# Prompt attention: both exponentials of a step ahead of the value copies, in tiles 4 to 7

## The reference, cut to what matters

```python
s_c = einsum(qg, kc);  p_c = masked_softmax(s_c, c_end <= q_pos)          # compressed blocks
s_s = einsum(qg, selected keys);  p_s = masked_softmax(s_s, k_pos <= q_pos)
s_w = einsum(qg, window keys);    p_w = masked_softmax(s_w, (dist >= 0) & (dist < WINDOW))
o = g0 * (p_c @ vc) + g1 * (p_s @ v_slc) + g2 * (p_w @ v_win)             # gates g
```

## Time and profile before

| | |
|---|---|
| median of 3 runs | 2177.78 us (2173.7 to 2178.57) |
| the profiled execution | 2175.42 us, of which the span is 2173.8 us |
| PE busy | 2087.7 us (96%) |
| DVE, ACT, POOL busy | 1160.8, 627.8, 168.7 us |
| chain that ended last | PE 88%, DVE 5%, ACT 4%, issue 1%, DMA 1% |
| line 1266 (exponentials) | 128 instructions, 88.9 us, on the chain 1% |
| line 1252 (value copies) | 148 instructions, 80.5 us, on the chain 1% |
| mean granted TensorE clock | 0.986 |

### The profile page before, as it was taken

One profiled execution on the slowest core, in us unless ns is written; L12 is line 12 of the kernel. 1 busy time (PEld: TensorE's weight loads), 2 busy tenths in 40 slices (PEclk: granted clock), 3 DMA queues, 4 the chain that ended last, 5 costly groups with the idle time before them and its releaser, 6 DMA issues.

```text
span 2173.8 us, 37161 instructions
## 1 busy us (share of the span) xinstructions
PE 2087.7 (96%) x15252; PEld 1186.4 (55%) x15252; DVE 1160.8 (53%) x2353; ACT 627.8 (29%) x1414; POOL 168.7 (8%) x280
## 2 busy tenths in 40 slices
PE   8999999899998897989998999999999999999999
PEld 6445566799997785444444444444444444444443
DVE  2035664376675556877656446354544545463635
ACT  5014553122231224766644222111111111111020
POOL 3000000122221101211203000000000000000000
PEclk9999999999998998999999999999999999999999
DMA  6100112100002731000036601111111111111112
GB/s 178 39 0 20 29 30 82 79 4 13 14 10 57 199 113 55 11 6 6 6 117 195 199 1 39 39 39 39 39 39 39 39 39 39 39 39 39 39 39 82
DMA packets 96886, 115.73 MB, mean 53 GB/s; under 512 B 32243, under 2 KB 68020, under 8 KB 96654
## 3 DMA queue, kind: packets, MB, share of 16 engines
q1 hardware_dynamic: 90702, 101.82, 14.9%
q10 hardware_dynamic: 4480, 7.34, 1.2%
q0 software_dynamic: 1536, 4.20, 0.6%
HBM read 104.75 MB, written 12.64 MB: 54 GB/s over the span
## 4 chain that ended last, share of the span: by engine, by line
PE 88%; DVE 5%; ACT 4%; issue 1%; DMA 1%; ACTq 0%; POOL 0%; POOLq 0%; DVEq 0%
PE psum L1396 81%; PE psum L1844 2%; PE psum L1728 1%; ACT arena L1266 1%; PE psum L1901 1%; ACT arena L1252 1%; DVE arena L2503 1%; DVE arena L2529 1%; DVE arena L2353 1%; PE psum L1646 0%; PE psum L1406 0%; ACTq L1217 0%; PE psum L2094 0%; DVE psum L2500 0%; DVE arena L2584 0%
## 5 line engine op out<-in xcount | busy, mean ns | idle before, releaser
L1396 PE MATMUL psum<-arena 64*64 64x64 f32 (+10 forms) x12296 | 1844.2, 347 | 51.6 <-ACT arena L1266 20.2
L1396 PEld LDWEIGHTS psum<-arena 64*64 64x64 f32 (+5 forms) x12296 | 959.8, 151 | 824.1 <-issue 652.0
L2701 DVE TENSOR_TENSOR arena<-arena,psum 128x512 f32<-128x512 f32 x51 | 35.1, 687 | 318.5 <-PE psum L1396 318.5
L1369 ACT ACTIVATE arena<-psum 128x512 f32<-128x512 f32 x51 | 30.3, 594 | 437.4 <-PE psum L1396 344.7
L1358 ACT ACTIVATE arena<-arena 128x512 f32<-128x512 f32 x64 | 40.2, 628 | 274.2 <-DVE arena L2715 168.0
L918 POOL TENSOR_TENSOR arena<-arena,m_lev 128x256 f32<-128x256 f32 x82 | 65.4, 798 | 574.3 <-DVE arena L2334 377.0
L1252 ACT ACTIVATE arena<-psum 128x512 f32<-128x512 f32 (+1 forms) x148 | 80.5, 596 | 68.3 <-PE psum L1844 60.3
L2503 DVE TENSOR_REDUCE arena<-psum 128x1 f32<-128x640 f32 (+7 forms) x128 | 84.6, 703 | 15.1 <-PE psum L1396 13.5
L1266 ACT ACTIVATE arena<-psum,arena 128x640 f32<-128x640 f32 (+7 forms) x128 | 88.9, 703 | 9.6 <-DVE arena L2503 9.5
L2353 DVE TENSOR_TENSOR arena<-arena,psum 128x512 f32<-128x512 f32 x65 | 44.6, 686 | 74.1 <-PE psum L1396 73.4
L1844 PEld LDWEIGHTS psum<-ident,arena 128*128 128x128 f32 x528 | 58.0, 143 | 45.5 <-issue 22.6
(11 more groups left out here) (314 smaller groups left out, 1787.6 us busy)
## 6 DMA issues: line engine op xcount, KB each, us to landing
arena<-in_w_up_dram SPq DMA_DIRECT2D x7, 2048.0 KB, 7.4
arena<-in_w_down_dram SPq DMA_DIRECT2D x7, 2048.0 KB, 7.8
arena<-in_cache_slc_kv_dram SPq DMA_DIRECT2D x96, 128.0 KB, 2.6
arena<-in_cache_cmp_kv_dram SPq DMA_DIRECT2D x72, 128.0 KB, 3.3
arena<-in_x_prompt_dram SPq DMA_DIRECT2D x16, 512.0 KB, 13.6
arena<-in_cache_cmp_kv_dram ACTq DMA_DIRECT2D x56, 128.0 KB, 3.4
arena<-in_w_in_dram SPq DMA_DIRECT2D x13, 512.0 KB, 3.8
arena<-in_w_in_dram SPq DMA_DIRECT2D x2, 2048.0 KB, 12.5
```

The lines of the kernel that those rows point to most:

```text
L1396: return nc.tensor.matmul(out, lhsT, rhs, start=start, stop=stop)
L2701: tt(u2, t_sb, bank_of(6), ALU.add).then_inc(sem("u_sum"), 1)
```

## The change

In a score step that is not the compressed one, in tile 4 or later, with no turn of queries before the next score step and exactly one value step there, both exponentials get keys x + 0.1 and x + 0.2, ahead of the copies of that value step (which is at x + 1). All other steps keep their keys. The copies keep their order among themselves, and so do the exponentials. Nothing is changed on PE, DVE, POOL or SP, and no wait is added or taken away.

```diff
             nxt = next((y for y in range(x + 1, len(order)) if order[y][0] == "S"), len(order))
             vs = [y for y in range(x + 1, nxt) if order[y][0] == "V"]
+            turns_queries = any(order[y][0] == "q" for y in range(x + 1, nxt))
+            if e[2] != "c" and UNITS_A[e[1]][0] >= WINDOW // P and not turns_queries and len(vs) == 1:
+                act_order += [(x + 0.1, ("E", e[1], e[2], 0)), (x + 0.2, ("E", e[1], e[2], 1))]
+                continue
             act_order.append((vs[0] + 0.5 if vs else x, ("E", e[1], e[2], 0)))
```

## The result

The changed kernel took **2165.62 us** (median of 5 runs, 2162.40 to 2165.74), where the kernel before took 2177.78 (5 runs by then, 2173.70 to 2182.02); ratio 0.9946, 95% interval 0.9931 to 0.9960. The profiled execution took 2165.64 us, with a span of 2164.0, against 2175.42 and 2173.8.

A forecast was written before the change was run, and what follows sets the result against it. PE was taken as the bound in tiles 4 to 7, waiting for exponentials queued behind early copies on ACT. Terms 1.88 + 3.52 + 0.99 + 0.67 + 0.30 made about 7.4: 2177.8 - 7.4 = 2170.4 us, range 2166.5 to 2176.5.

The forecast's parts named there:

- its term: Predicted gains of units 8 to 15, in order: 1.88, 1.49, 0.99, 0.87, 0.67, 0.53, 0.30 and 0.63 us.
- M + 0.86: In a 640-column step, the first exponential starts 0.86 us after M, the start of the pair of maxima.
- M + 1.63: In a 640-column step, the second exponential starts 1.63 us after the start of the pair of maxima.
- P at M + 2.57: In 640-column steps, P, the start of piece 0 of the next scores, comes at 2.57 instead of 3.20: gain 0.63 us.
- 2.90 at 768: In 768-column steps of unit 10, piece 0 of the next scores comes at 2.90 against 3.38: gain 0.48 us.
- 3.27 and 3.65: Piece 0 of the next scores at 896 and 1024 columns, against 3.59 and 3.81: gains 0.32 and 0.16 us.
- DVE's mask: First steps of units 9, 11, 13: mask ends at 945.65, so the next maxima start at most 0.24 us earlier.
- a sum of 7.36: Gain over tiles 4 to 7: 1.88 + 3.52 + 0.99 + 0.67 + 0.30 us, all taken to the kernel's end.
- The unknown cost: Exponentials of 640 to 1024 columns running while DVE reads the other strip: at most 0.01 us each, taken as 0.
- the third rival: Exponential and maximum take turns on PSUM in the changed steps: 5.0 us slower, 2182.8 us; chance 5%.
- The first: Gains of units 8, 10, 12, 14 (3.84 us) turn into longer stalls at unit ends: 2174.3 us; chance 15%.
- The second: In the changed steps the order changes and nothing moves: exponentials start as now or PE waits for copies; 2177.8 us, 5%.

The follow-up runs named there:

- experiment 11: The changed kernel once more, unchanged, 12 runs: 2167.82 us, ratio 0.9968 to the kernel before.
- 4: The changed kernel again, unchanged, 5 runs: 2166.53 us, ratio 0.9962 to the kernel before.
- 5: The changed kernel with only the first exponential ahead of the two copies, the second behind them: 2183.27 us, ratio 1.0035 to the kernel before.
- 7: The changed kernel, with the second exponential straight behind the first also in two-value steps of tiles 4 to 7 without a turn of queries next: 2164.80 us.
- 12: The changed kernel with the second exponential also moved in two-value steps, run once more, 5 runs: 2161.99 us, ratio 0.9933 to the kernel before.
- 2: The changed kernel with the move only in its 10 steps of 640 columns: 2169.12 us, ratio 0.9978 to the kernel before.
- 3: The changed kernel with the move only in its 6 steps of 768 to 1024 columns: 2173.17 us, ratio 0.9992 to the kernel before.
- 6: The changed kernel with the move also in one-value steps of tiles 4 to 7 with a turn of queries next: 2170.33 us, ratio 0.9975.
- 9: The changed kernel without the limit to tiles 4 to 7, so 17 more steps in tiles 0 to 3: 2169.04 us, ratio 0.9968.
- 10: The changed kernel with a PE pad, 28 repeated transposes in 3.2 us at the end of prompt attention: 2170.63 us, ratio 0.9981 to the kernel before.

## Why the prediction was wrong, and where it was right

**The steps.** The mechanism held, and each unit's gain came within 0.06 us of its term. M + 0.86 was measured, M + 1.63 came at 1.65, P at M + 2.57 in 640 steps came at 2.57 to 2.58, 2.90 at 768 at 2.92, 3.27 and 3.65 at 896 and 1024 at 3.28 and 3.65. The steps are 3.82 apart (3.81). DVE's mask is the next bound in unit 9: the gain there is 1.51, not the 1.79 that it would be without it (0.54 + 0.63 + 0.62). The stretch gained 7.33 us for a sum of 7.36. The sum has a slip: 3.17, 3.20 and 3.19 less 2.57 each make 1.85 in unit 8 and not 1.88, so it should read 7.33. That this is the measured figure to the last digit is luck, for single units are off by up to 0.06 in both directions.

**The unknown cost.** The overlap of exponential and running maximum was taken at nothing. Grouped by shape over the stretch of the changed kernel:

```profile
L1270 ACT ACTIVATE arena<-psum,arena 128x640 f32<-128x640 f32 x40 | 31.6, 794 | 13.3 <-DVE arena L2507 13.3
L2507 DVE TENSOR_REDUCE arena<-psum 128x1 f32<-128x640 f32 x40 | 31.1, 819 | 4.4 <-PE psum L1400 3.8
...
L1270 ACT ACTIVATE arena<-psum,arena 128x1024 f32<-128x1024 f32 x8 | 9.0, 1122 | 5.4 <-DVE arena L2507 5.4
```

The means, 794, 819 and 1122 ns, were 799, 820 and 1121 in the old order. That refutes the third rival. It could have been ruled out beforehand: the prediction says that no row of the kernel before shows the overlap at 640 columns and more, but at 1024 columns one does. The pair of maxima runs until 1048.48, and the first exponential, 0.89 us of it beside the second maximum, takes as long as the one that follows alone at 1048.68 (1.10 us):

```profile
1047.59 1.10 ACT L1266 ACTIVATE arena<-psum,arena 128x1024 f32<-128x1024 f32 x1
```

The Trainium skill ("PSUM — Partial Sum Buffer", "Specifications (TRN2)") says that ScalarE and VectorE reach PSUM side by side at full bandwidth if they don't collide in a bank. The trace agrees with it, now at 640 to 1024 columns.

**The other rivals.** The first falls with the table by unit: units 8, 10, 12 and 14 kept their 3.77 us, and the stall stayed at 0.66. The second falls with all of it.

**The step that failed** is "the forecast is for the median: 2177.8 - 7.4". It carried a gain that was right to 0.03 us on a base that wasn't.
- The three runs of before were a poor sample of it: 91 runs have a median of 2175.95. The profiled execution (2175.4), from which I moved the forecast away by 2.4 us, was the better base: 2175.95 - 7.33 = 2168.6, beside 2167.82 for experiment 11.
- The five runs of the changed kernel were a lucky sample of that: 2164.5 in the mean at a clock of 0.9878, where 22 runs have 2166.8 at 0.9870. Their median, 2166.53, would have stood just inside the range, at its lower edge. In the profiled execution the forecast of 2168.0 was missed by 2.4 us, and 2.48 stand ahead of the stretch, where the change does nothing. Within one kernel the time falls by 1.2 to 2.0 us for each 0.001 of mean granted clock (a straight line through the runs of each set with at least nine). At a clock of 0.986 the lines of the sets give 2174.6 to 2175.0 for the kernel before and 2167.1, 2169.1 and 2168.7 for the three sets of the changed one: 5.5 to 7.9 us, around the 7.33. Two of the three are sets of five runs with clocks of 0.987 to 0.989, so their lines are carried on beyond them; the twelve runs of experiment 11 against their own rounds give 2174.9 - 2168.7 = 6.2.
- The range was built on the cost terms alone. A run of one kernel stands anywhere within 10 to 14 us (2162.4 to 2172.0 for the changed kernel, 2170.8 to 2184.8 for the kernel before), and three of them don't fix a median to 2 us; that scatter belonged in the range.

**What stays open.** In the plain means the changed kernel is 9.2 us faster (22 and 91 runs), with a standard error of about 0.7, 1.9 more than its stretch. The surplus sits mostly in the sets of five runs: beside the gain of their stretches, the differences of the means from their own rounds are 5.5 (the first five), 2.3, 0.4, 1.3 and 5.2 us (experiments 4, 5, 7 and 12) in these, and between -0.7 and 1.2 in the six sets of nine to twelve runs (2, 3, 6, 9, 10 and 11, where for 10 the pad is counted in). The difference goes with the clock, and part of the clock's is shown to be chance (650 to 700 us). Whether the higher clock and the 2.4 us shorter sample stage belong to the new order isn't settled, nor why the stages behind it give up to all of that back: with the PE pad, standing 3 us later took about those 3 us, but no run moved it by the whole 7 with PE at work.

## What to carry to other kernels

In an in-order queue, ask of each entry how soon its result is wanted, and put the one that PE waits for ahead of the one whose result is used a step later; but move a whole group (half the move cost 8 us), and only where something long stands before the next use of what the moved entry frees (about 1 us lost per step otherwise). Work out such a move from one step's timeline: start of the maximum, its duration, the queue behind it, the release. Then put the forecast on a base with the run-to-run scatter in it, because here the scatter of the base was larger than the error of the whole sum.

## What the runs showed of the hardware that I had not expected

- The same instructions between 650 and 700 us ran at a granted clock of 0.86 in six executions and of 0.90 to 0.94 in eight, and prompt attention began between 825.98 and 831.50 us.
- With PE standing 6.67 us, the granted clock from 1100 to 1110 us was 0.60, and the kernel's mean lay 3.7 us (standard error about 0.9) further up than the 5.83 by which the first transposes behind the pad were delayed. With 3.2 us of transposes in that place it was 1.00, and no loss beyond the delay can be told (2.9 us in the mean for 3.06, standard error 1.2).
